# The units ahead of the delta layers reordered, gate masks read from PSUM, softmax scales folded into the queries

## The reference, cut to what matters

```python
q, k, v = jnp.split(silu(causal_depthwise_conv(dn_qkv, conv_w)), 3, axis=-1)
q, k = l2norm(q), l2norm(k)
beta = sigmoid(dn_b)
g = -exp(a_log) * softplus(dn_a + dt_bias)          # then a cumulative sum over each chunk
lmat = where(strict, einsum(k * beta, k) * decay, 0)
u, w = triangular_solve(lmat + I, [v * beta, k * beta * exp(g)])
```

## Time and profile before

| what | us |
|---|---|
| median of 3 runs (2304.57 to 2306.05) | 2304.69 |
| the profiled execution's own time | 2304.58 |
| its span, first to last instruction | 2302.7 |
| PE busy | 2258.6 (98%) |
| POOL busy | 1691.1 (73%) |
| ACT busy | 1088.4 (47%) |
| DVE busy | 1070.2 (46%) |
| mean granted clock of PE | 0.998 of full |

### The profile page before, as it was taken

The page is one execution under the profiler, slowest core; times in us unless marked ns, Lnnn a source line. Parts: engine busy times, 40 slices in busy tenths (PEclk is TensorE's granted clock), DMA queues, the critical chain, the costliest instruction groups (busy, mean ns, idle before and its releaser), DMA issues.

```text
span 2302.7 us, 41636 instructions
## 1 busy us (share of the span) xinstructions
PE 2258.6 (98%) x16611; PEld 2060.8 (89%) x16611; DVE 1070.2 (46%) x1874; ACT 1088.4 (47%) x1317; POOL 1691.1 (73%) x1337
## 2 busy tenths in 40 slices
PE   9999999999999999999999999999999999999998
PEld 8888999999988888899999998889898888898887
DVE  4334656323333333455553233334535765534766
ACT  5345444465434443464444734336655345565333
POOL 6998655556799899975555678996567997655996
PEclk9999999999999999999999999999999999999999
DMA  7654533334465555553343455565334556333553
GB/s 251 196 187 153 159 109 113 116 105 147 162 199 188 182 183 193 190 162 95 111 128 103 137 165 170 196 203 155 101 121 146 196 187 181 123 107 118 198 196 123
DMA packets 316572, 359.97 MB, mean 156 GB/s; under 512 B 20820, under 2 KB 295312, under 8 KB 316304
## 3 DMA queue, kind: packets, MB, share of 16 engines
q1 hardware_dynamic: 316074, 357.65, 48.1%
q10 hardware_dynamic: 358, 0.33, 0.0%
HBM read 356.91 MB, written 1.05 MB: 155 GB/s over the span
## 4 chain that ended last, share of the span: by engine, by line
PE 91%; DVE 4%; ACT 3%; POOL 1%; issue 1%; DMA 0%; SPq 0%; ACTq 0%; DVEq 0%
PE ps L800 24%; PE ps L611 21%; PE ps L643 17%; PE ps L648 9%; PE ps L677 4%; PE ps L930 1%; PE ps L912 1%; PE ps L1204 1%; PE ps L693 1%; POOL sb_lo L576 1%; PE ps L933 1%; PE ps L664 1%; PE ps L1256 1%; PE ps L839 1%; DVE sb_hT L1955 1%
## 5 line engine op out<-in xcount | busy, mean ns | idle before, releaser
L576 POOL TENSOR_TENSOR sb_lo<-sb_raw,sb_hi 128x512 fp32r<-128x512 f32 x1333 | 1690.9, 1304 | 594.0 <-ACT sb_hi L1363 592.4
L1363 ACT ACTIVATE sb_hi<-sb_raw 128x2048 fp32r<-128x2048 f32 (+2 forms) x341 | 639.0, 1875 | 740.1 <-PE ps L648 358.4
L643 PE MATMUL ps<-sb_hT,sb_hi 128*128 128x512 f32 x1792 | 426.1, 390 | 0.0
L643 PEld LDWEIGHTS ps<-sb_hT,sb_hi 128*128 128x128 f32 x1792 | 332.9, 188 | 66.4
L800 PE MATMUL ps<-sb_hT,sb_hi 128*128 128x256 f32 x2304 | 309.0, 288 | 4.5 <-DVE sb_hT L2219 2.8
L800 PEld LDWEIGHTS ps<-sb_hT,sb_hi 128*128 128x128 f32 x2304 | 284.9, 191 | 10.6 <-DVE sb_hT L2219 3.2
L648 PEld LDWEIGHTS ps<-sb_hT,sb_lo 128*128 128x128 f32 x1792 | 229.8, 191 | 8.7
L1967 DVE TENSOR_TENSOR sb_yinv<-ps,sb_row 128x512 f32<-128x512 f32 x112 | 77.5, 692 | 337.3 <-PE ps L648 336.4
L648 PE MATMUL ps<-sb_hT,sb_lo 128*128 128x256 f32 x1792 | 232.5, 283 | 0.0
L611 PE MATMUL ps<-sb_hi,sb_o_h 128*128 128x512 f32 x560 | 220.1, 393 | 0.4 <-DVE sb_o_l L1974 0.4
L611 PE MATMUL ps<-sb_hi,sb_o_l 128*128 128x512 f32 x560 | 218.9, 391 | 0.0
(11 more groups left out here) (403 smaller groups left out, 3363.1 us busy)
## 6 DMA issues: line engine op xcount, KB each, us to landing
sb_raw<-in_ffn_w_in SPq DMA_DIRECT2D x87, 1024.0 KB, 5.1
sb_raw<-in_w_in SPq DMA_DIRECT2D x76, 1024.0 KB, 5.2
sb_raw<-in_ffn_w_out SPq DMA_DIRECT2D x44, 1024.0 KB, 4.9
sb_raw<-in_ffn_w_up SPq DMA_DIRECT2D x44, 1024.0 KB, 5.1
sb_raw<-in_ffn_w_down SPq DMA_DIRECT2D x22, 1024.0 KB, 5.0
sb_raw<-in_w_out SPq DMA_DIRECT2D x16, 1024.0 KB, 5.2
sb_raw<-in_w_branch_a SPq DMA_DIRECT2D x8, 1024.0 KB, 5.2
sb_raw<-in_w_branch_b SPq DMA_DIRECT2D x8, 1024.0 KB, 5.2
```

Of the source, the lines that this page charges most:

```text
L576: ins = nc.gpsimd.tensor_tensor(lo[:, slot, c], raw[:, slot, c], hi[:, slot, c].bitcast(F32), ALU.subtract)
L643: mm(ps[:, bank + i, :].rearrange("p (h n) -> p h n", h=2), wh[:, c, i * P:(i + 1) * P], hT_both[:, :, c, :], start=c == 0, stop=False, sk ...
L1363: fn(hi[:, slot, 0:width], raw[:, slot, 0:width], ACT.Copy).then_inc(hi_ready, 1)
```

## The change

In words:

- `FIRST` is reordered: the gate unit a moves ahead of k, right behind b, and the last place is taken by sv 2 (values of the stick-breaking branch) instead of q 1; q 1 moves to the head of the first background list and sv 2 leaves it. Both lists keep their lengths.
- On PE, sv 2 runs after the 16 small turns, where the 20 empty transposes stood.
- DVE takes beta's sum and reciprocal ahead of a's row, k's evacuation behind "beg", v's behind the copy of the gate columns; q 1's evacuation moves into the delta layer. ACT runs `decays(0)` before the first background split, splits by the new numbers, and `silu_pair` waits for each unit just before its activation, in the order q, z, k, v.
- `lower` scales the Gram matrix by beta in PSUM first, needs no products of norms, applies inverse norm and decay in four instructions over 128x128 (out in PSUM), cuts the first level out of PSUM, and then copies the whole to SBUF; that copy carries the signal. The two `per_key` scalings become four instructions each.
- Softmax scales go into the queries: two tiny products on DVE at the start of the second layers' mixer, a scalar in existing instructions, and for the memory queries a scalar_tensor_tensor in place of a tensor_tensor. The maxima are negated by the reduction itself; L2486 goes.

```diff
-FIRST = [("sv", 0), ("sv", 1), ("q", 0), ("z", 0), ("b", 0), ("k", 0), ("a", 0), ("v", 0), ("q", 1)]
+FIRST = [("sv", 0), ("sv", 1), ("q", 0), ("z", 0), ("b", 0), ("a", 0), ("k", 0), ("v", 0), ("sv", 2)]
-DELTA_BG = [pair_units(1)[1:] + [("sv", 2), ("sv", 3), ("gb", 0)], pair_units(2) + [("sq", 0), ("sk", 0)],
+DELTA_BG = [pair_units(1) + [("sv", 3), ("gb", 0)], pair_units(2) + [("sq", 0), ("sk", 0)],
...
-                for r in range(3, len(FIRST)):
+                for r in range(3, len(FIRST) - 1):
                     unit1(l, b, r)
...
-                warm(2)
+                unit1(l, b, len(FIRST) - 1)
...
-                for u in pair_units(c):
-                    freed(l, MIX1_ORDER.index(u))
-                for buf in (kT, qT, vT, zT):
+                for kind, buf in (("q", qT), ("z", zT), ("k", kT), ("v", vT)):
+                    freed(l, MIX1_ORDER.index((kind, c)))
...
                 key_norms(0)
+                decays(0)
                 yield
-                decays(0)
...
-                mix_split(b, 8)
                 act.wait_ge(rows_dve, ROWS_DVE.at(l, "y"))
...
-                mix_split(b, 9)
+                mix_split(b, 8)
                 act.wait_ge(rows_dve, ROWS_DVE.at(l, "g"))
...
+                mix_split(b, len(FIRST))
                 mix_split(b, len(FIRST) + 1)
                 silu_pair(l, 0)
...
-                    wf("norms")
-                    tt(pairs(norms[:, 3, :]), column(0, c), pairs(norms[:, 1, :]), ALU.mult)
-                    tt(pairs(norms[:, 4, :]), column(0, c), pairs(norms[:, 2, :]), ALU.mult)
-                    own.link(tt(pairs(norms[:, 5, :]), column(2, c), pairs(norms[:, 2, :]), ALU.mult))
                     dve.wait_ge(fr_pe, FRONT_PE.at(NPAIR * l + c, "gram"))
-                    own.link(tt(four(ps[:, 2, :]), four(ps[:, 2, :]), per_key(4), ALU.mult))
+                    own.link(tt(tiles(ps[:, 2, :]), tiles(ps[:, 2, :]), along(0, c), ALU.mult))
+                    wf("norms")
                     wf("down")
-                    own.link(tt(lmat[:], lmat[:], ps[:, 2, :], ALU.mult))
+                    for p in range(4):
+                        n = slice(p * P, (p + 1) * P)
+                        ins = stt(out=ps[:, 2, n], in0=ps[:, 2, n], scalar=norms[:, 2, p:p + 1], in1=lmat[:, n], op0=ALU.mult, op1=ALU.mult)
+                    own.link(ins)
                     for h, rows in enumerate(ROWS):
-                        ins = tt(compact(p_half)[rows], four(lmat[rows, :])[:, :, h * H:(h + 1) * H], over(cc("inv0")[rows], 4), ALU.mult)
-                    ins.then_inc(fr_dve, 1)
+                        tt(compact(p_half)[rows], four(ps[rows, 2, :])[:, :, h * H:(h + 1) * H], over(cc("inv0")[rows], 4), ALU.mult)
+                    V.tensor_copy(lmat[:], ps[:, 2, :]).then_inc(fr_dve, 1)
+
+                def scaled(dst, bank, c, kind, root):
+                    for p, (i, t) in enumerate((i, t) for i in range(2) for t in range(ST)):
+                        n = slice(p * P, (p + 1) * P)
+                        ins = stt(out=dst[:, n], in0=ps[:, bank, n], scalar=tcol[:, kind, t, 2 * c + i:2 * c + i + 1],
+                                  in1=norms[:, root, p:p + 1].to_broadcast([P, P]), op0=ALU.mult, op1=ALU.mult)
...
-                            tt(four(u_v[:]), four(ps[:, 4, :]), per_key(3), ALU.mult)
+                            scaled(u_v, 4, c, 0, 1)
...
-                            tt(four(w_k[:]), four(ps[:, 3, :]), per_key(5), ALU.mult)
+                            scaled(w_k, 3, c, 2, 2)
...
-                evac1(l, b, 5)
-                dve.wait_ge(unit_done, RING * b + (A_AT + RING + 1))
-                ts(y, ps[h8, A_AT % 2, 0:S], hcol[:, 0:1], None, ALU.add).then_inc(rows_dve, 1)
...
+                dve.wait_ge(unit_done, RING * b + (A_AT + RING + 1))
+                ts(y, ps[h8, A_AT % 2, 0:S], hcol[:, 0:1], None, ALU.add).then_inc(rows_dve, 1)
...
-                evac1(l, b, 7)
+                evac1(l, b, FIRST.index(("k", 0)))
...
+                evac1(l, b, FIRST.index(("v", 0)))
                 dve.wait_ge(rows_dve, ROWS_DVE.at(l, "cols"))
-                with_units(delta(l), DELTA_PLAN, l, b, [(8, (0, 1))])
+                with_units(delta(l), DELTA_PLAN, l, b, [])
...
-                    sig(tt(qT[:, 2 * m:2 * m + 2, :], two(ps[:, 6 + m, :]), over(row[:], 2), ALU.mult))
+                    sig(stt(out=qT[:, 2 * m:2 * m + 2, :], in0=two(ps[:, 6 + m, :]), scalar=P ** -0.5, in1=over(row[:], 2), op0=ALU.mult, op1=ALU.mult))
...
-                own.link(V.tensor_reduce(negmax[:, w, :], ps[:, 2 * w:2 * w + 2, :].rearrange("p b (t n) -> p (b t) n", n=S), AX_X, ALU.max))
-                sig(ts(negmax[:, w, :], negmax[:, w, :], -float(dk) ** -0.5, None, ALU.mult))
+                sig(V.tensor_reduce(negmax[:, w, :], ps[:, 2 * w:2 * w + 2, :].rearrange("p b (t n) -> p (b t) n", n=S), AX_X, ALU.max, negate=True))
```

More of the change, by code:

```diff
@@ L1822, in mixer2 @@
                 order = scores_order(M2_BATCHES)
-                softmaxes = attention([order[0], order[2], order[1]] + order[3:], wp, wv, sig, lambda n: (MLA_DK if n < 3 else 64) ** -0.5,
+                softmaxes = attention([order[0], order[2], order[1]] + order[3:], wp, wv, sig,
                                       (qT[:, 4:8, :], zT[:, 0:4, :]), (4, 4), early, lambda: out_highs(0, 2))
@@ L1828, in mixer2, with attention @@
                 out_highs(2, 4)
-            def attention(order, wp, wv, sig, scale, pts, bank, after, last=None):
+            def attention(order, wp, wv, sig, pts, bank, after, last=None):
                 for step in order:
@@ L1839, in attention @@
                             ins = fn(pbuf[:, i * S:(i + 1) * S], ps[:, 2 * w + i // ST, (i % ST) * S:(i % ST + 1) * S], ACT.Exp,
-                                     bias=negmax[:, w, i:i + 1], scale=scale(beta), accum_out=psum_p[:, w, i:i + 1])
+                                     bias=negmax[:, w, i:i + 1], accum_out=psum_p[:, w, i:i + 1])
                         sig(ins)
@@ L1865, in out_high @@
                     sig(fn(o_h[:, 2 * beta:2 * beta + 2, :], two(ps[:, 2 * beta, :]), ACT.Copy))
-                for _ in attention(ME_ORDER, wp, wv, sig, lambda n: P ** -0.5, (kT[:, 4:8, :], zT[:, 0:4, :]), (4, 6), out_high):
+                for _ in attention(ME_ORDER, wp, wv, sig, (kT[:, 4:8, :], zT[:, 0:4, :]), (4, 6), out_high):
                     pass
@@ L2083, in delta @@
                 compact = lambda v: v.rearrange("p (k n) -> p k n", n=H)
-                pairs = lambda v: v.rearrange("p (i t) -> p i t", i=2)
-                per_key = lambda i: norms[:, i, :].unsqueeze(2).to_broadcast([P, 4, P])
                 def column(kind, c):
@@ L2371, in mixer2 @@
                 two = lambda v: v.rearrange("p (k n) -> p k n", n=S)
+                ts(gcol[:, 1:3], vec2[:, V2_CQ:V2_CQ + 2], float(MLA_DK) ** -0.5, None, ALU.mult)
+                own.link(ts(gcol[:, 3:4], v2(V2_GQ), 64 ** -0.5, None, ALU.mult))
                 for g in range(4):
@@ L2393, in mixer2 @@
                 for j in range(4):
-                    ins = stt(out=qT[:, j, :], in0=qT[:, j, :], scalar=v2(V2_GK if j == 3 else V2_GQ), in1=roots[:, 2 + j, :], op0=ALU.mult, op1=ALU.mult)
+                    ins = stt(out=qT[:, j, :], in0=qT[:, j, :], scalar=v2(V2_GK) if j == 3 else gcol[:, 3:4], in1=roots[:, 2 + j, :], op0=ALU.mult, op1=ALU.mult)
                 sig(ins)
                 for k in range(3):
-                    ins = stt(out=zT[:, k, :], in0=zT[:, k, :], scalar=v2(V2_CQ + k), in1=roots[:, (0, 0, 1)[k], :], op0=ALU.mult, op1=ALU.mult)
+                    ins = stt(out=zT[:, k, :], in0=zT[:, k, :], scalar=v2(V2_CKV) if k == 2 else gcol[:, 1 + k:2 + k], in1=roots[:, (0, 0, 1)[k], :], op0=ALU.mult, op1=ALU.mult)
                 own.link(ins)
@@ L2443, in top @@
                 def top(beta):
-                    maxima(beta, wp, sig, MLA_DK if beta < 3 else 64)
+                    maxima(beta, wp, sig)
                 top(0)
@@ L2496, in memory @@
                     two = lambda v: v.rearrange("p (k n) -> p k n", n=S)
-                    sig(tt(qT[:, 2 * m:2 * m + 2, :], two(ps[:, 6 + m, :]), over(row[:], 2), ALU.mult))
+                    sig(stt(out=qT[:, 2 * m:2 * m + 2, :], in0=two(ps[:, 6 + m, :]), scalar=P ** -0.5, in1=over(row[:], 2), op0=ALU.mult, op1=ALU.mult))
                 for beta in range(ME_BATCHES):
-                    maxima(beta, wp, sig, P)
+                    maxima(beta, wp, sig)
                 for beta in range(ME_BATCHES):
```

5 lines of the change are left out of this document (3 added, 2 removed).

## The result

The changed kernel takes 2288.39 us (median of 4 runs, 2287.82 to 2289.2) against 2305.37 us for the kernel before on the same chip (4 runs, 2304.57 to 2306.7). The ratio is 0.9928, 95% interval 0.9917 to 0.994. The gain is 17.0 us where 11.9 were summed. The profiled execution after took 2288.66 us, with a span of 2286.1.

A forecast was written before the change was run, and what follows sets the result against it. PE, busy 98% of the span, was taken as the bound. Terms 4.3 + 1.6 + 3.1 + 0.9 - 0.4 + 1.0 + 1.4 = 11.9 us off 2304.6, plus 0.1 to the median, gave 2292.8 us, range 2289 to 2298.

The forecast's parts named there:

- Rivals 1, 3 and 4: PE: 1, late activation or scan, 2295.8, chance 0.15; 3, transposes covered a chain, 2300.7, 0.06; 4, scalings await POOL, 2319, 0.04.
- rival 4: Levels 2 and 3 of each pair: the 64 new scalings each wait for POOL; 2319 us, chance 0.04.
- softmax term: Memory attention and mixer: shorter DVE chains cut PE's waits by 1.0 and 1.4 us in two layers.
- first level: PE's mask waits ahead of L902: 3.1 us go whole, less 0.4 charged for the scalings, 2.7 in both layers.
- sum of squares: PE's wait at L884, later pairs: the shorter DVE chain ends it, 0.9 us in two layers.
- units ahead of the delta layer: PE up to L856: empty transposes at full clock 4.3 us and the bank wait 1.6, 5.9 in both layers.
- a ahead of k: Gate unit moved before k: v 0 no longer waits for k 0's bank, 0.8 us per layer, 1.6 in all.
- Rival 2: Stretch behind the small turns: the clock drops in both layers, 2294.5 us, or in none, 2291.1; chance 0.15.

The follow-up runs named there:

- old chain: Kernel after with DVE's first-level chain and the two scalings as before, the units' order staying changed; 2290.23 us.
- masks from SBUF: Kernel after with the scaled matrix copied to SBUF first and the two masks cut from SBUF behind it; 2289.64 us, one run.
- the old softmax: Kernel after with the softmax part undone: maxima scaled in a second instruction, scale in the exponential, none in the queries; 2294.8 us.
- memory and mixer edits: Two runs against the kernel after: without empty transposes in the memory attention, 2292.13 us; with ten added in the mixer's wait, 2287.67 us.
- empty transposes back: Kernel after with the 20 empty transposes put back on PE, behind sv 2 and ahead of the delta layer; 2293.89 us.
- the old order: Kernel after with a behind k again and DVE's order to match, beta's sum and reciprocal behind a's row; 2294.22 us.

## Why the prediction was right and wrong

**Right.** What the prediction was surest of held: the delta layer's front follows sv 2 at once, the waits of L800, L902 and L884 are gone, and no new one of over 1 us came. The bank was free for v 0 with 0.8 us in hand (0.4 said), the mask takes 0.42 us, and the scalings 0.34 each (0.3 to 0.45 said). Rivals 1, 3 and 4 are out: no wait came in the transposes' place, putting them back costs their whole length, and DVE is 9 us less busy rather than 51 more. On rival 4 the Trainium skill's page "SBUF — State Buffer" (Who interferes with whom) held in this trace: all 64 scalings of L2116, with one input tensor in PSUM and one in SBUF, took 340 to 345 ns, whether POOL was at work or idle. The prediction gave the page's rule without its exception, "outside the 2-port perf modes", which the page says a tensor_scalar can enter. The trace agrees with that too: L2094 is a tensor_scalar with one input, in SBUF, and took 1.55 us with POOL at work and 0.43 with POOL idle.

**Wrong.** The step that failed is the sum's softmax term, 2.4 us, which measured 5.4. Two readings of rows went into it. The wait of L1087 for ACT stood in the earlier trace rows once, and half was taken for the other layer. The kernel has it in both (0.95 us each, and 1.1 by the starts); the execution shown had run that piece at half clock and so without the wait. And behind it lay gains that the term left out: in each mixer 0.2 us over the next three batches, and 0.5 us around the fifth, of which the list of waits shows 0.27 (L1256, from 2.8 to 2.2 in total). In the memory attention the first chain is shorter by 0.36 and not 0.2, the second batch by 0.48 and not 0.3. The three rows summed to 5.5, which the text gave as the upper end; the range took in only 1.5 above the term.

The other terms were each a little low and all on the same side: first level 3.4 for 2.7, since the scalings cost nothing on PE's path where 0.4 was charged, and the whole wait with a little beside it went; sum of squares 1.43 for 0.9; units ahead of the delta layer 6.26 for 5.9. Each is 0.4 to 0.7 us, together 1.6. The range was built as if these would scatter.

**The first level** came out for another reason than the sum gave. It set q 1's evacuation, products and masks against the wait together. With the old chain in the new order the wait is gone as well, so the order does it alone, and the chain pays at L884. The prediction carried the masks' 1.68 us over as their price, but in the new order the masks from SBUF take 0.85, as much as from PSUM: that reading held for a place beside POOL's work, and the order moved it.

**a ahead of k** was counted at the 1.6 us of its row. Measured in the new order, and together with beta's place, it is 3.6, because a second wait, for "beg", stood hidden behind the first. Part of what the sum put down to the transposes hangs on it.

**The clock.** One half-clock stretch behind the turns was assumed in two layers. The profiled execution had none there and one at 1630, for 1.6 us; the next profile of the same kernel had both. Rival 2 was right about chance: seven profiles of kernels with sv 2 right behind the sixteen turns and nothing behind it but the delta layer (the old softmax, old chain, masks from SBUF, memory and mixer edits and the two of the kernel itself) show it in 5 of 14 places. With the two others in which sv 2 follows the sixteen turns (empty transposes back, where the clock falls ahead of the transposes, and the old order), it is 9 of 18. It decided the last microsecond of single runs, not the 17 us: before against after, both without any stretch, is 16.9.

## What to carry to other kernels

Before taking a term from one wait row, look whether the same place in the other layer ran at full clock: a stretch at half clock swallows a wait, and the row that is missing is a gain that is there. Where a chain loses an instruction, count what it saves in every batch up to the whole of the listed waits, and let the upper end of the range be that whole. Empty matmuls are to be judged by place: in front of ready work they cost their length, in a wait they cost nothing, and the kernel without them in two waits was 3.7 us longer here, 3.0 of it at half clock behind the waits. And a DVE duration taken from a row holds for what POOL did beside it: after a change of order, look where POOL works.

## What the runs showed of the hardware

- After 1.9 us of sixteen matmuls of 8 columns, in a stream that is busy throughout, the granted clock fell to 0.50 (as 0.50 and 0.65 in 252 to 256) in some executions and not in others of the same kernel; each time cost 1.4 to 1.7 us. With 48 such matmuls it fell in both layers of the one profile, while they still ran.
- A wait of 3.1 us of PE was followed by half clock in both memory attentions, in the one profile taken, and the four runs of that kernel lie within 0.4 us. With twenty transposes in most of the wait and 0.95 us of it left, nine profiles show none there (18 places); with 1.3 us left, three of eight places do.
- A tensor_scalar from SBUF to SBUF over 128x512 (L2094, L2095) took 1.03 to 1.55 us where POOL was at work when it began (31 of 31) and 0.41 to 0.43 where POOL was idle (193 of 193). The products L2116 that read PSUM took 340 to 345 ns in either case. No run varied POOL's work alone, so the cause rests on this sorting.
